# The order of high and low matmuls within a weight chunk, in a float32 decoder layer

## What is computed

```python
h = rmsnorm(x, g_mix[i])
proj = h @ w_in[i]
...
mixed = jax.nn.sigmoid(gate_a) * y_a + jax.nn.sigmoid(gate_b) * y_b
x = x + mixed @ w_out[i]
h = rmsnorm(x, g_ffn[i])
x = x + (jax.nn.silu(h @ w_ffn_gate[i]) * (h @ w_ffn_up[i])) @ w_ffn_down[i]
h = rmsnorm(x, g_ple[i])
x = x + jax.nn.sigmoid(h @ w_ple_gate[i]) * (p[i] @ w_ple_proj[i])
```

## Time and profile before

| what | value |
|---|---|
| median of 3 runs | 1536.12 us (1535.49 to 1536.4) |
| profiled execution | 1536.4 us, span of its instructions 1534.6 us |
| PE busy | 98% of the span |
| DVE, ACT, POOL busy | 64%, 48%, 8% |
| DMA queue of the weights | 59.4% of 16 engines' span, 275.78 MB |
| mean granted clock | 0.994 |

### The profile page before, as it was taken

One profiled execution on the slowest core, in us unless ns is written; L12 is line 12 of the kernel. 1 busy time (PEld: TensorE's weight loads), 2 busy tenths in 40 slices (PEclk: granted clock), 3 DMA queues, 4 the chain that ended last, 5 costly groups with the idle time before them and its releaser, 6 DMA issues.

```text
span 1534.6 us, 25491 instructions
## 1 busy us (share of the span) xinstructions
PE 1504.8 (98%) x8805; PEld 1332.4 (87%) x8805; DVE 986.6 (64%) x1194; ACT 741.5 (48%) x967; POOL 126.3 (8%) x175
## 2 busy tenths in 40 slices
PE   5999999999999999999999999999999999999997
PEld 4888998888988888888888888888888888888886
DVE  6976676667666776776666666656665555455765
ACT  6544435544444665554444444444444444444554
POOL 4011101100111000220000000000000011001031
PEclk9999999999999999999999999999999999999998
DMA  5666575555655565566665656666565665556553
GB/s 137 203 187 173 149 235 164 163 174 179 184 161 167 187 196 186 173 197 186 188 192 173 200 183 191 185 192 191 179 197 179 188 201 176 187 187 202 167 165 110
DMA packets 278124, 277.56 MB, mean 181 GB/s; under 512 B 13048, under 2 KB 275648, under 8 KB 277696
## 3 DMA queue, kind: packets, MB, share of 16 engines
q1 hardware_dynamic: 277632, 275.78, 59.4%
q10 hardware_dynamic: 448, 1.19, 0.2%
HBM read 274.83 MB, written 2.11 MB: 180 GB/s over the span
## 4 chain that ended last, share of the span: by engine, by line
PE 96%; DVE 2%; DMA 1%; ACT 0%; issue 0%; ACTq 0%; DVEq 0%
PE acc L1174 57%; PE acc L1183 30%; PE side L1174 2%; PE acc L1295 1%; PE acc L1294 1%; PE acc L1293 1%; PE side L1183 1%; DVE hn L779 1%; DMA rope_c<-in_rope_rows 1%; PE side L1306 0%; DVE ls L723 0%; PE side L1312 0%; PE side L1320 0%; PE side L1321 0%; PE side L1305 0%
## 5 line engine op out<-in xcount | busy, mean ns | idle before, releaser
L723 DVE TENSOR_TENSOR ls<-ws,hs 128x1024 fp32r<-128x1024 f32 (+2 forms) x528 | 642.8, 1232 | 423.6 <-ACT hs L418 415.3
L418 ACT ACTIVATE hs<-ws 128x1024 fp32r<-128x1024 f32 (+2 forms) x528 | 541.8, 1039 | 522.6 <-PE acc L1183 289.8
L1174 PE MATMUL acc<-xg,hs 128*128 128x512 f32 x1664 | 408.0, 392 | 0.6 <-DVE y_ple L1095 0.6
L1174 PEld LDWEIGHTS acc<-xg,hs 128*128 128x128 f32 x1664 | 302.2, 189 | 56.9 <-DVE y_ple L1095 1.0
L1174 PE MATMUL acc<-hn,hs 128*128 128x512 f32 x1072 | 271.0, 396 | 5.7 <-DVE hn L779 5.7
L1183 PEld LDWEIGHTS acc<-xg,ls 128*128 128x128 f32 x1664 | 221.0, 191 | 12.5
L1174 PEld LDWEIGHTS acc<-hn,hs 128*128 128x128 f32 x1072 | 194.6, 190 | 42.3 <-DVE hn L779 6.6
L1183 PE MATMUL acc<-xg,ls 128*128 128x256 f32 x1664 | 226.2, 283 | 0.0
L1174 PE MATMUL acc<-ff,hs 128*128 128x512 f32 x704 | 176.4, 392 | 0.0
L1183 PEld LDWEIGHTS acc<-hn,ls 128*128 128x128 f32 x1072 | 145.3, 192 | 9.7 <-DVE hn L779 0.6
L1183 PE MATMUL acc<-hn,ls 128*128 128x256 f32 x1072 | 151.1, 286 | 0.3 <-DVE hn L779 0.3
(11 more groups left out here) (226 smaller groups left out, 1136.7 us busy)
## 6 DMA issues: line engine op xcount, KB each, us to landing
ws<-in_w_in SPq DMA_DIRECT2D x152, 512.0 KB, 4.1
ws<-in_w_ffn_gate SPq DMA_DIRECT2D x88, 512.0 KB, 4.5
ws<-in_w_ffn_up SPq DMA_DIRECT2D x88, 512.0 KB, 4.5
ws<-in_w_ffn_down SPq DMA_DIRECT2D x64, 512.0 KB, 3.6
ws<-in_w_out SPq DMA_DIRECT2D x32, 512.0 KB, 4.6
ws<-in_w_ple_gate SPq DMA_DIRECT2D x32, 512.0 KB, 4.7
ws<-in_w_ffn_down SPq DMA_DIRECT2D x32, 384.0 KB, 3.7
ws<-in_w_o_b SPq DMA_DIRECT2D x16, 512.0 KB, 3.5
```

What stands on the lines that cost most here:

```text
L418: act.activation(hs[:, j, 0:n], ws[:, j, 0:n], ACT.Copy).then_inc(h_split, 1)
L723: dve.tensor_tensor(ls[:, j, 0:n], ws[:, j, 0:n], hs[:, j, 0:n].bitcast(F32), ALU.subtract).then_inc(l_split, 1)
L1174: mm = pe.matmul(acc_of(bank + m, 2 * TOK), hs[:, j, at], src[:, k, :], start=first and q == 0, stop=last and q == len(tiles) - 1)
```

## The change

`consume` no longer has a high part and a low part. It waits once, for `l_split` of the chunk (which comes after `h_split`), and then goes through `m` and `q` and issues for each weight tile its long and its short matmul one after the other. The short one stands second, except for the last tile of an accumulation, where it stands ahead of the long one that has `stop=True`. The wait for `h_split` is gone from PE. The number, shapes and operands of the matmuls stay the same, and nothing is changed on other engines.

```diff
-            rows = range(banks) if tile is None else (tile,)
-
-            def high_part(some):
-                pe.wait_ge(h_split, 4 * u + j + 1)
-                for m in rows:
-                    for q, k in some:
-                        at = slice(q * width + m * P, q * width + (m + 1) * P)
-                        mm = pe.matmul(acc_of(bank + m, 2 * TOK), hs[:, j, at], src[:, k, :],
-                                       start=first and q == 0, stop=last and q == len(tiles) - 1)
-                return mm
-
-            def low_part():
-                pe.wait_ge(l_split, 4 * u + j + 1)
-                for m in rows:
-                    for q, k in enumerate(tiles):
-                        at = slice(q * width + m * P, q * width + (m + 1) * P)
-                        mm = pe.matmul(acc_of(bank + m, TOK), ls[:, j, at], src[:, k, 0:TOK], start=False, stop=False)
-                return mm
-
-            pieces = list(enumerate(tiles))
-            if last:
-                if first:
-                    high_part(pieces[:1])
-                low_part()
-                mm = high_part(pieces[1:] if first else pieces)
-            else:
-                high_part(pieces)
-                mm = low_part()
+            pe.wait_ge(l_split, 4 * u + j + 1)
+            for m in range(banks) if tile is None else (tile,):
+                for q, k in enumerate(tiles):
+                    at = slice(q * width + m * P, q * width + (m + 1) * P)
+                    begins, ends = first and q == 0, last and q == len(tiles) - 1
+                    high, low = (hs[:, j, at], src[:, k, :]), (ls[:, j, at], src[:, k, 0:TOK])
+                    whole, half = acc_of(bank + m, 2 * TOK), acc_of(bank + m, TOK)
+                    if ends:
+                        pe.matmul(half, *low, start=False, stop=False)
+                        mm = pe.matmul(whole, *high, start=False, stop=True)
+                    else:
+                        pe.matmul(whole, *high, start=begins, stop=False)
+                        mm = pe.matmul(half, *low, start=False, stop=False)
```

## The result

The changed kernel takes 1548.81 us (median of 4 runs, 1548.62 to 1549.17) against 1536.09 us: +12.7 us, a ratio of 1.0084 with a 95% interval of 1.0069 to 1.0098. It is slower. The time lies just inside the range of 1523 to 1549 us, but the forecast was 1532, faster, and that it lies inside is luck (see "Why the prediction was wrong").

The account below looks back on a forecast made before the run. PE's matmuls were taken as the bound. 3984 pairs at 347.7 instead of 348.65 ns gave -3.8 us: 1532.6 from the profiled 1536.4, and 1532 against the median of 1536.12; range 1523 to 1549 us.

Parts of the forecast that it names:

- What bounds the kernel: Whole kernel: PE is busy for 98% of the span, so time is number of matmuls times the slot, start to start.
- steps (1) to (3): Work and other queues unchanged; waiting for `l_split` ahead of the chunk costs nothing, at worst 1.2 us once; slots freed as before.
- The sum of before: Old order: 3984 long-short pairs, about 390 switches at 20 ns net, 348.65 ns a pair on the mean, 1389 us.
- Step (4), the price of a pair: Alternating long and short matmuls on PE: 347.7 ns a pair, bounded by 345.5 and 350.7, so -3.8 us.
- The upper bound: Alternating pair on PE: long slot 232.5 ns plus short slot 118.2, its gift spread over four shorts, together 350.7 ns.
- The reasons for the low side: Why 347.7 ns, under the middle: the first short holds most of the gift; settled slots would sum to 346.7 ns.
- A sum that a settled alternation would also reach: Alternating pair on PE: both settled slots cost N/2.4 + 13.3 ns, 226.7 and 120, together 346.7 ns.
- four late `ls`: Range's upper end: PE waiting for four late L723 of 1.2 us each, one for each slot, above 1544 us.
- The one that the alternation never settles: Rival for the alternation on PE: every long stays slow, shorts get part of their gift; 350.7 ns, +8.2 us, 1544; chance 0.34.
- The one by which order tells nothing: Rival: a pair on PE keeps 348.65 ns in either order, 1536 us; chance 0.14.
- The signs of being wrong: Prediction wrong if a pair is far outside 345.5 to 350.7 ns, or 36 to 1412 us doesn't carry nearly all the difference.
- The other sign: Prediction wrong if the stretch from 36 to 1412 us, 90% of the time, doesn't carry nearly all of the difference.

## Why the prediction was wrong

- **What bounds the kernel; steps (1) to (3).** Right. PE is busy all through, no engine or queue became the bound, and the wait for `ls` costs nothing (0.9999). That ACT's waits would grow by the same microseconds as the span was not exact: 18.4 against 12.3.
- **The sum of before.** Right in kind and size: runs of 16 save 20 ns for each switch taken away (2.7 us expected, 3.0 measured).
- **Step (4), the price of a pair.** This is the step that failed. I took 347.7 ns, between 345.5 and 350.7. Over its pairs `after` has 235.0 + 117.0 = 352.0 ns against 348.8 before (slots that end in a wait or in other work left out), and 3984 times the difference, 3.24 ns before rounding, are 12.9 us, as good as the whole 12.7. The upper bound was too low for one reason: I built it from a long slot's mean loss of 6 ns in the first four of a run. In the slow pattern the long slots are 232, 241 and 236, a mean loss of 9.7 ns. In uninterrupted runs of `before` no long slot is over 236. The short slots, 118, 120 and 113, lie within the bounds with their mean of 117.
- **The reasons for the low side.** The first one, that most of a run's gift belongs to its first short matmul, failed: in either pattern a short one keeps a mean gift of some 3 ns and not of 7. "A sum that a settled alternation would also reach" is true of the fast pattern (346.7), and it holds in `w_ffn_down`. Wrong was the silent step that there is one settled state. There are two, and which one comes is set by what was issued before.
- **The range.** It reached 1549 us only by four late `ls` of 1.2 us each on top of the 1544 of the upper bound. They cost nothing, so it was luck that this width covered an error that lay elsewhere.
- **The rivals.** The one that the alternation never settles came nearest, on its side and with its mechanism in part (each long stays slow), but with 1544 us it too was short. The one by which order tells nothing is refuted by twelve kernels of the same matmuls between 1532.5 and 1550.2 us, the kernel with 512 columns left aside.
- **The signs of being wrong.** A pair outside the bounds is what the feed-forward stage shows, 353.3 ns over 350.7. The other sign stayed away: the stretch to 1412 us carries nearly all of the difference, since the matmul that starts at 1414.1 us in `before` starts 11.9 us later in `after`.

Shown: the cause is the order of the two lengths, and neither the wait nor the bank nor the change of weight tile; equal lengths have no loss; a pattern is held from one irregular place to the next. With two pairs between the places the fast one follows, with one or three the slow one; this was so from 503 us on, from the merge to the end of `w_ffn_down`, but for the first one to three units behind an interruption or behind another order. Open: what in TensorE carries the state from one matmul to the next, and so a rule that would name the pattern for an order not yet tried; one place a unit led to both patterns in turn. That the interruptions of the attention restart the slow pattern was seen in the trace and was not tried by itself.

## What to carry to other kernels

Where PE is the bound, take the slot (start to start) of each kind of matmul from the timeline and not its duration, and count what a change of length costs: here 20 ns for each switch from 512 columns to 256 and back, in runs of six or more. Keep matmuls of one length together in runs as long as the buffers allow; doubling the runs was one line and gave 0.2%. A price for an order that no trace shows can't be put together from the edges of another order: measure a short kernel of that order first, and look whether its slots repeat.

## What was not expected of the hardware

- An alternation of 512 and 256 columns has two stable prices, 346.7 and 353.3 ns a pair, which hold for up to 86 pairs until an irregular place; one pair moved in a unit's last chunk turns one into the other, worth 7.7 us of 475 in the feed-forward stage.
- Long matmuls right after a change of length took up to 242 ns where 227 is the settled slot, at a granted clock of 1.00 and with no wait.
- Within a run of equal lengths the settled slot was N/2.4 + 13.3 ns: 227 for 512 columns, also with the two weight tiles in turn, and 120 for 256.
